# A hybrid attention and mixture-of-experts block: the second expert's rows prepared like the first's, a ninth buffer for raw weights, and VectorE's order at the entry changed

## What is computed

```python
def expert_block(args):
    xb, e = args                       # up to 128 rows of v that chose expert e
    return (jax.nn.silu(xb @ w_gate[e]) * (xb @ w_up[e])) @ w_down[e]

y = jnp.zeros((N + 1, D), hf.dtype).at[row_tok].add(y_rows * row_gate[:, None])
h = h + y
```

## Time and profile before

| what | value |
| --- | --- |
| median of 3 runs | 1247.57 us (1247.12 to 1248.65) |
| the profiled execution | 1247.12 us, span of its instructions 1244.5 us |
| TensorE matmul busy | 1176.6 us (95%) |
| VectorE busy | 866.5 us (70%) |
| ScalarE busy | 734.3 us (59%) |
| GpSimd busy | 278.0 us (22%) |
| DMA | 288.12 MB, mean 232 GB/s |
| mean granted TensorE clock | 0.983 |

### The profile page before, as it was taken

One profiled execution on the slowest core, in us unless ns is written; L12 is line 12 of the kernel. 1 busy time (PEld: TensorE's weight loads), 2 busy tenths in 40 slices (PEclk: granted clock), 3 DMA queues, 4 the chain that ended last, 5 costly groups with the idle time before them and its releaser, 6 DMA issues.

```text
span 1244.5 us, 17640 instructions
## 1 busy us (share of the span) xinstructions
PE 1176.6 (95%) x6164; PEld 962.1 (77%) x6164; DVE 866.5 (70%) x975; ACT 734.3 (59%) x894; POOL 278.0 (22%) x249
## 2 busy tenths in 40 slices
PE   5999999999999998999978999999999999999993
PEld 4897787877767776777867888888888878888882
DVE  6721112276556697677678989988888889898881
ACT  5532222366454593222456788877877878788870
POOL 3300000010000001223333233344443332122220
PEclk9999999999999999999988999999999999999997
DMA  7155523020000132466588999999999999999971
GB/s 261 44 203 186 182 114 110 1 69 18 18 13 22 38 141 78 144 237 251 214 329 309 360 376 373 377 375 365 374 385 375 377 375 376 379 377 389 377 250 16
DMA packets 67828, 288.12 MB, mean 232 GB/s; under 512 B 13008, under 2 KB 20193, under 8 KB 43202
## 3 DMA queue, kind: packets, MB, share of 16 engines
q1 hardware_dynamic: 51538, 238.30, 50.4%
q0 software_dynamic: 10864, 30.29, 9.0%
q10 hardware_dynamic: 5376, 18.88, 3.9%
HBM read 242.79 MB, written 48.25 MB: 234 GB/s over the span
## 4 chain that ended last, share of the span: by engine, by line
PE 38%; DMA 12%; DVE 6%; ACT 2%; issue 1%; POOL 0%; ACTq 0%; POOLq 0%; DVEq 0%
DMA raw<-in_expert_w_up 12%; PE banks L742 11%; PE banks L744 11%; PE banks L743 11%; DVE ew_l L1556 3%; ACT ew_h L1385 2%; PE banks L1078 1%; PE banks L987 1%; PE banks L1109 1%; PE banks L978 1%; DVE masked L1764 1%; PE banks L911 1%; PE banks L924 0%; PE banks L1059 0%; PE banks L957 0%
## 5 line engine op out<-in xcount | busy, mean ns | idle before, releaser
L1556 DVE TENSOR_TENSOR ew_l<-raw,ew_h 128x2048 fp32r<-128x2048 f32 x192 | 437.8, 2290 | 63.3 <-ACT ew_h L1385 61.6
L1385 ACT ACTIVATE ew_h<-raw 128x2048 fp32r<-128x2048 f32 x192 | 367.9, 1919 | 106.8 <-PE banks L744 47.9
L742 PE MATMUL banks<-ew_h,xb_h 128*128 128x512 f32 x512 | 203.5, 397 | 9.7 <-DVE xb_l L1556 7.8
L744 PE MATMUL banks<-ew_h,xb_l 128*128 128x512 f32 x512 | 200.3, 391 | 0.0
L743 PE MATMUL banks<-ew_l,xb_h 128*128 128x512 f32 x512 | 199.8, 390 | 0.0
L1682 DVE TENSOR_TENSOR_SCAN tails<-tails 128x512 f32<-128x512 f32 (+3 forms) x96 | 94.0, 1020 | 62.6 <-ACT tails L1351 62.4
L742 PE MATMUL banks<-win_h,u_h 128*128 128x512 f32 (+1 forms) x320 | 122.5, 383 | 2.8 <-DVE u_l L1556 2.5
L742 PEld LDWEIGHTS banks<-ew_h,xb_h 128*128 128x128 f32 x512 | 96.7, 189 | 31.5 <-issue 12.5
L743 PE MATMUL banks<-win_l,u_h 128*128 128x512 f32 (+1 forms) x320 | 118.7, 371 | 0.0
L744 PE MATMUL banks<-win_h,u_l 128*128 128x512 f32 (+1 forms) x320 | 118.7, 371 | 0.0
L744 PEld LDWEIGHTS banks<-ew_h,xb_l 128*128 128x128 f32 x512 | 96.4, 188 | 20.7
(11 more groups left out here) (241 smaller groups left out, 1987.1 us busy)
## 6 DMA issues: line engine op xcount, KB each, us to landing
raw<-in_expert_w_gate SPq DMA_DIRECT2D x64, 1024.0 KB, 11.8
raw<-in_expert_w_up SPq DMA_DIRECT2D x64, 1024.0 KB, 8.5
raw<-in_expert_w_down SPq DMA_DIRECT2D x64, 1024.0 KB, 12.8
rows_dram<-zero_rows ACTq DMA_DIRECT2D x8, 2048.0 KB, 7.6
win_raw<-in_w_in SPq DMA_DIRECT2D x16, 512.0 KB, 5.2
x_in<-in_x SPq DMA_DIRECT2D x8, 512.0 KB, 9.9
raw<-in_w_out SPq DMA_DIRECT2D x4, 1024.0 KB, 5.3
h_row<-in_x SPq DMA_DIRECT2D x8, 512.0 KB, 6.3
```

Of the source, the lines that this page charges most:

```text
L742: mm(ps, lh, rh, start=start, stop=False)
L744: return mm(ps, ll, rh, start=False, stop=stop)
L1385: A(ew_h[slot % SPLIT][:, :], raw[raw_slot][:, :], ACT.Copy).then_inc(ew_h_ready, 1)
L1556: return V.tensor_tensor(dst, src, high.bitcast(fp32), SUB)
```

## The change

Second block's rows: its slots are loaded into `xb_second` (over `gain2`) before tile 7 is scattered, transposed behind block 0's gate and up, and tile 7's rows are added by a third one-hot matrix. Down of block 0 is split: its second half now runs behind gate and up of block 1, so pieces are numbered anew (4 is down 0's first half, 5 to 8 gate and up of expert 1, 9 down 0's second half; from 10 on as before). A ninth raw buffer, two pieces (7, 8) requested before the last tile's stores, buffers and slots in another order. ScalarE makes high parts 0 to 2 earlier and loads the silu table ahead; VectorE makes low 1 before the last tile's mean, low 2 before `x_low(0)`, and `count_blocks` moves behind low 10; the marks of empty slots become a step of their own (`skip_empty`) with its own count of `control_ready`. The gathers of rows 2 and 3 take their indices from `source` directly, 128 of them. Cut to its core:

```diff
+RAW_OF = (1, 2, 3, 8, 4, 5, 0, 1, 2, 6, 7, 3, 4, 5, 0, 1, 2, 6, 7, 3, 4, 5)
+FIRST_LOADS = (0, 1, 4, 5, 6, 2, 3)
+EW_AT = (4, 0, 2, 1, 3, 5)
...
+        raw.append(at(f"raw{RAW + 2}", M + 16 * KB, [P, PIECE]))
+        xb_second = at("xb_second", R3 + 16 * KB, [P, D])
...
 SyncE
             for t in range(TILES):
+                if t == TILES - 1:
+                    load_behind(7, 0)
+                    load_behind(8, 1)
                 sp_e.wait_ge(v_ready, t + 1)
...
+                if t == 6:
+                    sp_e.wait_ge(g_kv, 2 * TILES)
+                if t < len(FIRST_LOADS):
+                    load(FIRST_LOADS[t])
...
+            sp_e.wait_ge(v_turned, TILES)
+            for k in range(2):
+                sp_e.wait_ge(h_stored[k], 16 * TILES // 2)
+            load(9)
+            sp_e.wait_ge(ranked, TILES)
+            sp_e.wait_ge(v_stored[0], 16 * TILES // 2)
+            sp_e.wait_ge(own_scattered[0], 32 * TILES // 2)
+            load(10)
+            load_behind(11, 2)
+            for m in range(12, 22):
+                load_behind(m, m - 8)
 GpSimd
-            for t in range(TILES - 2, TILES):
-                scatter_own(t)
-                if t < TILES - 1:
-                    scatter_given(t)
+            scatter_own(TILES - 2)
+            scatter_given(TILES - 2)
+            pool.wait_ge(own_scattered[0], 32 * TILES // 2)
+            pool.wait_ge(own_scattered[1], 32 * (TILES - 2) // 2)
+            pool.wait_ge(v_ready, TILES)
+            nc.gpsimd.dma_start(xb_second[:, :], own_dram[P:2 * P, :]).then_inc(second_in, 16)
+            pool.wait_ge(second_in, 16)
+            scatter_own(TILES - 1)
             for i in range(2):
                 pool.wait_ge(own_scattered[i], 32 * TILES // 2)
-            pool.wait_ge(x_turned, 1)
-            nc.gpsimd.dma_start(xb[:, :], own_dram[P:2 * P, :]).then_inc(rows_in, 16)
             scatter_given(TILES - 1)
...
-            pool.wait_ge(control_ready, 1)
-            pool.wait_ge(x_turned, 2)
-            gather(2)
+            pool.wait_ge(control_ready, SOURCE)
+            pool.wait_ge(logit_done, TILES)
+            gather_early(2, xb, rows_in)
...
             pool.wait_ge(x_turned, 3)
-            gather(3)
+            gather_early(3, xb, rows_in)
+            pool.wait_ge(control_ready, CONTROL)
             pool.wait_ge(y_ready, 1)
 TensorE
-                    if k == 6 and t == TILES - 1:
+                    if k == 5 and t == TILES - 1:
                         rank_tile(TILES - 2)
...
-                    if j == 1 and not whole:
+                    if j == 0 and not whole:
                         count_all()
+                    if j == 2 and between is not None:
+                        between()
...
             gate_up(0, (0, 0))
+            for half in range(2):
+                first_rows(half, True, xb_second)
             turn_act(0)
-            down(0, (4, 4), first=True, between=lambda: turn_rows(1))
-            gate_up(1, (6, 0))
-            turn_rows(2)
+            for half in range(2):
+                last = add_rows(TILES - 1, half, column=2)
+            last.then_inc(x_turned, 1)
+            down(0, (4, 4), first=True, parts=(0,))
+            gate_up(1, (5, 5), between=lambda: turn_rows(2))
+            down(0, (8, 2), first=True, parts=(1,))
             turn_act(1)
 ScalarE
                 if w == TILES - 1:
-                    act.wait_ge(g_mixed, TILES)
-                    high(0, 0, raw_slot(0), raw_count(0), guard=False)
+                    act.wait_ge(v_turned, TILES - 1)
+                    for m in (1, 2):
+                        high(m, m, raw_slot(m), raw_count(m), guard=False)
...
+                if w == TILES - 2:
+                    act.wait_ge(g_mixed, TILES)
+                    high(0, 0, raw_slot(0), raw_count(0), guard=False)
...
                 act.wait_ge(x_turned, i + 1)
+                if isinstance(i, int) and i == 2:
+                    act.wait_ge(ew_used, 9)
...
             x_high(0)
-            high(5, 5, raw_slot(5), raw_count(5), guard=False)
+            nc.scalar.preload_act_table_set("silu_and_others")
             high(6, 6, raw_slot(6), raw_count(6))
+            act.wait_ge(ew_l_ready, 4)
             silu_of(0)
-            high(7, 7, raw_slot(7), raw_count(7))
+            for m in (7, 8):
+                high(m, m, raw_slot(m), raw_count(m))
             a_high(0)
-            for m in (8, 9):
-                high(m, m, raw_slot(m), raw_count(m))
+            high(9, 9, raw_slot(9), raw_count(9))
             x_high(1)
 VectorE
+                if t == TILES - 1:
+                    key = hot_key[:, 2:3]
+                    link(V.scalar_tensor_tensor(out=key, in0=chosen_any[:, t, 1:2], scalar=FAR, in1=bank[7][:, 257:258],
+                                                op0=MUL, op1=ADD))
+                    V.tensor_scalar(hot[2][:, :], iota[:, :], FAR, key, ADD, ALU.is_equal).then_inc(hot_ready, 1)
...
             add_h(TILES - 1)
+            low_piece(1, 1, raw_slot(1))
             mean_h(TILES - 1)
...
+            low_piece(2, 2, raw_slot(2))
             x_low(0)
-            for m in (1, 2, 3, 4, 5):
+            low_piece(3, 3, raw_slot(3))
+            skip_empty()
+            for m in (4, 5, 6):
                 low_piece(m, m, raw_slot(m))
-            count_blocks()
             activate(0, 4)
             a_low(0)
-            for m in (6, 7):
+            low_piece(7, 7, raw_slot(7))
+            x_low(1)
+            for m in (8, 9, 10):
+                low_piece(m, m, raw_slot(m))
+            count_blocks()
+            activate(1, 9)
+            x_low(2)
+            for m in (11, 12):
                 low_piece(m, m, raw_slot(m))
+            a_low(1)
+            low_piece(13, 13, raw_slot(13))
             find_extra()
-            low_piece(8, 8, raw_slot(8))
-            x_low(1)
-            low_piece(9, 9, raw_slot(9))
+            for m in (14, 15):
+                low_piece(m, m, raw_slot(m))
...
-            step(1)
+            step(2)
```

More of the change, by code:

```diff
@@ L223, in hybrid_block_kernel @@
         start_at, level = nxt("start_at", EXTRA), nxt("level", EXTRA)
-        hot = [nxt(f"hot{i}", P) for i in range(2)]
+        hot = [nxt(f"hot{i}", P) for i in range(3)]
         hot_key = nxt("hot_key", 8)
@@ L458, in _, with load, load_behind @@
             sp_e.wait_ge(wo_l_ready, 4)
+            def load(m):
+                if m in (4, 9):
+                    src = down_v[0][:, PIECE * (m // 9):PIECE * (m // 9 + 1)]
+                elif m < 10:
+                    src = gate_up(0, m) if m < 4 else gate_up(1, m - 5)
+                else:
+                    i, j = (m + 2) // 6, (m + 2) % 6
+                    src = gate_up(i, j) if j < 4 else down_v[i - 1][:, PIECE * (j - 4):PIECE * (j - 3)]
+                load_piece(raw_slot(m), src)
+            def load_behind(m, low):
+                sp_e.wait_ge(ew_l_ready, low + 1)
+                load(m)
             for t in range(TILES):
+                if t == TILES - 1:
+                    load_behind(7, 0)
+                    load_behind(8, 1)
                 sp_e.wait_ge(v_ready, t + 1)
@@ L1079, in turn_rows, with gate_up @@
                 last.then_inc(x_turned, 1)
-            def gate_up(i, m0):
+            def gate_up(i, m0, between=None):
                 count, slot0 = m0
@@ L1110, in turn_act, with down @@
                 last.then_inc(a_turned, 1)
-            def down(i, m0, first=False, between=None):
+            def down(i, m0, first=False, parts=(0, 1)):
                 count, slot0 = m0
@@ L1117, in down @@
                     pe.wait_ge(y_ready, i)
-                for j in range(2):
+                for j in parts:
                     pe.wait_ge(ew_l_ready, count + j + 1)
@@ L1480, in down_value @@
             def down_value(i):
-                return 6 if isinstance(i, int) and i == 0 else 6 * i + 10
+                return 6 * i + 10
             def a_high(i):
@@ L1945, in step @@
                     low_piece(6 * i + 4, 4, 0)
-                activate(i, 10 if isinstance(i, int) and i == 1 else 6 * i + 2)
+                activate(i, 6 * i + 2)
                 if not last:
```

101 lines of the change are left out of this document (45 added, 56 removed).

## The result

The changed kernel takes **1257.27 us** (median of 5 runs, 1256.33 to 1258.73), the kernel before 1248.43 us in the 5 runs beside it (1247.12 to 1250.71). The ratio is **1.0066, 95% interval 1.0051 to 1.008**: slower by some 8 us, where 5.3 us of gain were forecast, and outside the range.

What follows compares the result with a forecast made beforehand. Bounds: weight splitting on VectorE and ScalarE, TensorE's turns with 7.0 us lost to DMA, a near-bound weight stream, and TensorE's entry waits. The larger lead, 5.3, gave 1247.57 - 5.3 = 1242.3 us; range 1237.5 to 1247.5.

Steps and rivals of the forecast that it cites:

- the check of GpSimd's part: GpSimd's entry chain, tile 6's scatter to block 2's gather: landed 660.1, wanted by TensorE at 660.9, slack 0.8.
- rival B: Block 2's gather late by 2.4, or 6.1 with the VectorE-GpSimd port locked (landing 667.0); 1244.7 to 1248.4; chance 0.16.
- Rival D: Four serial GpSimd landings meet pieces 7 to 11; TensorE waits 9.7 in block 1's gate and up; 1252.0; chance 0.10.
- Step 1: Entry of block 0: x_low(0) starts at 633.9, gate and up at 634.7, 1.2 later than 633.51.
- Step 2: Block 0: activate(0) follows gate and up at once; TensorE turns its activations at 647.0, not 650.30.
- Step 3: Block 1: eight one-hot products take half of 4.09; gate and up start at 652.7 instead of 662.43.
- Step 4: Block 2: on TensorE's side gate and up could start at 667.8, 10.2 before 678.06.
- Step 5: Blocks 2 and 3: VectorE cannot follow; block 3's gate and up start at 691.4 against 697.49, 6.1 earlier.
- Step 6: Entry clock: two close waits of about 3 us cost 1.7, bounds 0 and 3.4; lead entering block 4 is 4.4.
- Step 7: Weight stream: piece 22 lands at 689.3, 5.3 ahead of 694.5; later requests 4 to 6 us earlier, DMA full.
- the sum: Whole kernel: the stream's lead of 5.3, larger than TensorE's 4.4, moves the end by 5.3, to 1242.3.
- rival C: Weight stream doesn't gain: piece 22 lands within 1 or 2 us of 694.5, DMA retakes the lead; 1246; chance 0.06.

Runs made afterwards that it cites:

- experiment 4: Changed kernel with weight pieces 7 and 8 requested only once the first block's early rows have landed; 1254.46 us, ratio 1.005.
- 8: Changed kernel with pieces 7 and 8 held for the first rows, piece 9 onward for the second rows, and VectorE's other order; 1252.96 us, ratio 1.0035.
- experiment 12: Changed kernel with requests held for first rows, second rows and tile 7's scatters, early gather before table scatters, VectorE reordered, x_low(3) before low 19; 1243.71 us, ratio 0.9964.
- experiment 14: Kernel of experiment 12 with VectorE's order put back to the changed kernel's own; 1245.1 us, ratio 0.9985.
- 2: Changed kernel with piece 9 and all pieces behind it requested only after the second rows have landed; 1250.67 us, ratio 1.0034.
- experiment 1: Changed kernel with tile 7's two table scatters moved behind the early gather for block 2; 1251.33 us, ratio 1.0015.
- 7: Changed kernel with piece 9 onward held until the second rows land, low 11 before activate(1), and find_extra behind block 2's step; 1248.34 us, ratio 0.9999.
- 9: Changed kernel with piece 9 onward held for the second rows, VectorE's other order, and x_low(3) ahead of low 19; 1247.26 us, ratio 0.9999.
- 5: Changed kernel with only VectorE's entry reordered: low 11 before activate(1), find_extra behind block 2's step, GpSimd's wait for it one gather later; 1256.99 us, ratio 1.0078.
- 10: Changed kernel without early second rows (loaded whole behind all scatters), with piece 9 onward held until they land; 1246.33 us, ratio 0.9986.
- 13: Kernel of experiment 12 without early second rows: loaded whole after all own scatters land, third one-hot matrix removed; 1242.96 us, ratio 0.997.
- 3: Changed kernel without early second rows and third one-hot matrix: rows loaded whole once tile 7's scatters have landed; 1255.09 us, ratio 1.0062.

## Why the prediction was wrong

**The step that failed** is the check of GpSimd's part, "the gather 660.1, the slack is 0.8". By its own terms:

| term | forecast | measured |
| --- | --- | --- |
| last scatter of tile 6 ends | 624.1 | 627.51 |
| its landing | 3.95 | 9.5 |
| load of the second rows, landing (issue included) | 7.6 | 9.2 |
| tile 7's two scatters, landing | 2.3 + 7.6 | 3.6 + 8.8 |
| its table scatters | 4.3 | 3.3 |
| gather, landing | 2.64 + 7.6 | 2.3 + 7.5 |
| gather landed | 660.1 | 671.66 |

Of the 11.6 us, 5.6 are tile 6's landing: I took 3.95 from the kernel before, where it is the landing of tile 7's scatter. In the trace of before, DMA is only 0.37 busy at 634 to 638, as that scatter lands. The change fills just such room; a landing read beside an idle queue was used beside a full one. 3.4 come from two landings that I did not put on the list at all. Tile 5's scatter lands 6.45 after its issue, where it took 5.33; piece 3 now goes out beside it, and holding 7 and 8 (experiments 4, 8) leaves it at 6.3 and 6.4. The first rows, with 3 and 7 in front of them, release tile 6's scatter 6.6 after their own issue instead of 4.3; in experiment 4 it is 4.3 again. The rest is 1.6 and 2.5 on the next two steps, less 1.5 on the last two. I took 7.6 where rows offered 9.3, and for one place the smaller number still. A slip in rival B is small: 7.6 in place of 3.95, less the slack of 0.8, is 2.9 and not 2.4.

**Rival D** had the mechanism (four landings in series beside the pieces, a wait in gate and up of block 1), the gather's landing (670.6; measured 671.66) and the sum (1252.0; measured 1257.27, still short). The wait was 6.47, not 9.7, since TensorE also asked later, at 665.19 instead of 660.9. It got 0.10 because I judged it by the landings of before. The forecast moved SyncE's requests earlier and counted that as a gain for the stream, and did not ask, for each of them, which small transfer was then under way.

Step by step:

- **Step 1**, entry at 634.7: measured 637.29, and 634.69 in experiment 4, where the first rows do not meet pieces 7 and 8. The work was sized right; the wait of 1.94 and what led to it were missing.
- **Step 2**, turn of block 0 at 647.0: 649.64 after; 647.0 in experiment 4, 646.6 in 8.
- **Step 3**, gate and up of block 1 at 652.7: 656.81, 5.6 ahead of before instead of 9.7; 2.6 come from step 1, and 1.9 from a term that I sized wrong: the 4.09 of the earlier trace rows, which I halved, are the products of one tile already, sixteen of them, and the change adds sixteen again, 3.97 instead of 2.05. It is so in every run with early rows.
- **Step 4**, gate and up of block 2 could start at 667.8: 681.1. This is the failed check: of the 13.3, 6.5 are the wait, 4.1 come from step 3, and 2.7 is the lower clock behind the wait (9.06 from the third rows' transposes to turn 1, 6.36 in experiment 12, where there is no wait).
- **Step 5**, VectorE as the next bound, with waits of 2.8 and 3 at activate(2) and x_low(3): right in place and size, 2.63 and 2.46 after and 2.64 and 2.83 in experiment 14, where no transfer is late. Gate and up of block 3 start at 693.80 there; forecast 691.4.
- **Step 6**, 1.7 of clock: 2.2 after (22.4 from turn 2 to 3, less 17.75, less the wait of 2.46); 2.7 in experiments 2 and 14. Two further waits also cost clock, which I had not counted: behind the 6.47 the products came each 0.43 us for a while instead of 0.23.
- **Step 7** and the sum: experiment 14, the nearest to my forecast, has a lead of 1.1 at turn 3 where step 6 gave 4.4, and 1.1 and 2.8 at turns 8 and 31. The lead is gone ahead of the stream: gate and up of block 3 start 3.7 early instead of 6.1, and the clock takes 2.7 instead of 1.7. Experiment 12 has 7.9 at turn 3 and loses 5.7 to the wait at block 4 and the clock behind it. Piece 22 lands at 690.7 in experiment 14 (asked for at 685.3, 5.4 later), against 694.5 before and 689.3 forecast, so rival C is not borne out. The ratio of 14, 0.9985, is a gain of 1.9 where 5.3 was forecast.

**The port of VectorE and GpSimd.** Of the indirect issues that fell beside low parts, the first scatter of tile 7 took 2.30 where one alone takes 0.98, the second table scatter 1.90, the gather 1.97 (1.05 alone); the longest such issue in the entry of any run is the gather of experiments 12 and 14, 3.17. VectorE's low parts beside them, three in a row each time:

```profile
640.95 6.69 DVE L1599 TENSOR_TENSOR ew_l<-raw,ew_h 128x2048 fp32r<-128x2048 f32 x3
656.57 6.69 DVE L1599 TENSOR_TENSOR ew_l<-raw,ew_h 128x2048 fp32r<-128x2048 f32 x3
```

The first row ends at 647.64 and the scatter at 648.50; the second ends at 663.26 and the gather at 664.18; the low part ahead of that ends at 661.1 and the table scatter at 661.91. An indirect issue that begins beside a low part ends 0.84 to 0.93 behind that part's end, here and in the entries of all the runs. The Trainium skill, "SBUF — State Buffer", section "SBUF: two separate sides", would allow each to wait a whole low part; the trace agrees with the lock, but the wait is only what is left of the low part: here it was 1.3 at most, and 2.1 in the entry of any run. The load of the second rows, a direct one, took 0.58, and in the kernel before 0.57 beside a low part. The estimate made by that rule, a gather landed at 667.0, lay nearer than mine, but for another reason: the lateness came from landings, not from issues. In experiment 12 these waits are 4.8 us of the chain (issues of 2.77, 1.87 and 3.17).

**What stays open.** Inside a late landing the runs do not tell queueing behind the packets of pieces from packets that take longer. Tile 6's landing, still 10.3 in experiment 12, was not held free by itself, and the stores of tile 7, which go out beside it, were not moved. The gain of each hold of 12 alone is not measured, nor is most of what the gather first gave in experiment 1 explained.

## What to carry to other kernels

Before bulk loads are asked for earlier, list the small transfers that depend on each other in that stretch, and price each landing beside a full DMA, not from a trace where the DMA was idle just then; with three or four in series a slack of a few us is none. Gate the bulk requests on the landing of the whole dependent chain, last link included: holding them for one link only moves the collision to the next. And when TensorE leaves an entry earlier while another engine's queue has little to spare, reordering that queue may only choose the block that waits: of the waits of 2.64 and 2.83 in experiment 14, 12 has one left, 2.59 at block 4.

## What was not expected of the hardware

- The same load of 512 KB of rows landed 3.7 to 3.95 us after its issue with the requests for pieces held (experiments 2, 7, 8, 9, 12, 14) and in 8.6 to 9.0 with pieces 10 and 11 asked for within 0.5 us of it (after, 1, 4, 5). The scatters of tile 7 landed in 3.05 to 3.22 (10, 12, 14; 4.34 in 13) and in 8.8 to 12.3 with pieces let go beside them (after, 1 to 5, 7 to 9).
- A wait of 2.5 to 2.9 us of TensorE, with another short one ahead of it or not, was followed by a granted clock that fell to 0.50 to 0.73 over 5 us (after and experiments 1 to 5, 7, 8, 10, 12 to 14), and the turn was 1.8 to 3.1 us longer than 17.75 and the wait together. In experiment 9 a wait of 2.58 at block 4 cost only 0.3 more, with the clock at 1.00 from 715 to 720; in experiment 12 one of 2.59 at the same block cost 3.1, with the clock at 0.50 from 710 to 715. The same wait has no fixed price.
